# Expert layers in 32-token blocks on four column groups, blocks placed by expert rank in both layers, rows moved four blocks at a time

## The reference, cut to what matters

```python
grp = argmax(h @ w_coarse)                       # 1 of 4 groups
top_val, top_idx = top_k(fine logits of grp, 2)  # 2 of its 8 experts
gate = softmax(top_val) * w_grp
expert = grp * 8 + top_idx                       # 32 experts in all
def run_block(xe, e):                            # rows sent to expert e
    return (silu(xe @ w_gate[e]) * (xe @ w_up[e])) @ w_down[e]
y[token] += run_block(...) * gate                # each token gets 2 rows
```

## Time and profile before

| what | value |
| --- | --- |
| median of 3 timed runs | 1810.76 us (1804.28 to 1812.93) |
| the profiled execution | span 1805.0 us from first to last instruction; its time outside the span is not listed, and the three timed runs lie 0.7 us below to 7.9 us above this span |
| TensorE busy | 1687.1 us, 93% of the span |
| VectorE, ScalarE, GpSimd busy | 661.3, 448.8, 170.2 us |
| mean granted TensorE clock | 0.965 |
| moved by DMA | 519.45 MB, 288 GB/s over the span |
| layer 0, first turned block to last scatter | 353.4 to 875.8 us |
| layer 1, first turned block to last scatter | 1281.0 to 1776.1 us |

### The profile page before, as it was taken

How to read it: one execution, slowest core, us unless ns; L and a number is a source line. 1 busy time by engine, 2 the same in 40 slices (tenths; PEclk the granted TensorE clock), 3 DMA queues, 4 the chain that set the end, 5 groups by cost and what they waited for, 6 DMA issues and landing times.

```text
span 1805.0 us, 21821 instructions
## 1 busy us (share of the span) xinstructions
PE 1687.1 (93%) x8694; PEld 870.0 (48%) x8694; DVE 661.3 (37%) x1266; ACT 448.8 (25%) x807; POOL 170.2 (9%) x172
## 2 busy tenths in 40 slices
PE   7999999799999999999699998999699999999983
PEld 3455454445445555555345458965333333333331
DVE  3279341432222213122469846542522222221213
ACT  2233671133221112211448403332000000000001
POOL 0000000011111111110000113100111111111100
PEclk9999999799999999999899998999799999999996
DMA  9265531499999999999560181055899999999995
GB/s 366 98 238 183 195 133 47 141 401 408 394 408 408 403 411 403 403 413 394 191 239 1 25 124 48 1 211 219 317 397 403 398 409 406 406 416 413 420 421 197
DMA packets 95324, 519.45 MB, mean 288 GB/s; under 512 B 22509, under 2 KB 28237, under 8 KB 70648
## 3 DMA queue, kind: packets, MB, share of 16 engines
q1 hardware_dynamic: 84024, 500.66, 71.3%
q0 software_dynamic: 11200, 17.39, 2.9%
HBM read 508.19 MB, written 29.15 MB: 298 GB/s over the span
## 4 chain that ended last, share of the span: by engine, by line
PE 72%; DMA 12%; issue 8%; DVE 5%; ACT 2%; SPq 2%; DVEq 0%; POOLq 0%
PE bank L865 24%; PE bank L881 11%; PE bank L458 8%; PE bank L466 8%; DMA ring<-in_w_up 7%; PE bank L852 3%; PE bank L822 3%; PE bank L892 2%; PE bank L524 2%; PE bank L689 2%; PE bank L451 1%; DVE arena L2622 1%; PE bank L731 1%; DMA ring<-diag 1%; DMA arena<-xnd,smalli 1%
## 5 line engine op out<-in xcount | busy, mean ns | idle before, releaser
L867 PE MATMUL bank<-ring,arena 128*64 128x512 f32 x912 | 412.5, 606 | 0.0
L865 PE MATMUL bank<-ring,arena 128*64 128x512 f32 x896 | 402.5, 603 | 7.4 <-DMA ring<-in_w_up 4.9
L2521 DVE TENSOR_TENSOR arena<-arena,bank 64x512 f32<-64x512 f32 x70 | 48.3, 690 | 556.8 <-ACT arena L1815 556.8
L458 PE MATMUL bank<-arena,ring 128*128 128x512 f32 x560 | 244.6, 593 | 0.0
L865 PEld LDWEIGHTS bank<-ring,arena 128*64 128x64 f32 x896 | 119.6, 139 | 242.7 <-issue 236.0
L881 PE MATMUL bank<-ring,arena 128*64 128x512 f32 x424 | 195.0, 603 | 0.0
L883 PE MATMUL bank<-ring,arena 128*64 128x512 f32 x424 | 194.9, 603 | 0.0
L1815 ACT ACTIVATE arena<-bank 64x512 f32<-64x512 f32 x70 | 41.2, 588 | 509.6 <-PE bank L867 509.6
L1454 POOL DMA_INDIRECT arena<-xnd,smalli x70 | 67.6, 966 | 1052.6 <-PE bank L852 531.6
L458 PEld LDWEIGHTS bank<-arena,ring 128*128 128x128 f32 x560 | 105.4, 190 | 126.9 <-issue 126.9
L466 PE MATMUL bank<-arena 128*128 128x128 f32 x1008 | 126.8, 279 | 0.0
(11 more groups left out here) (441 smaller groups left out, 2110.0 us busy)
## 6 DMA issues: line engine op xcount, KB each, us to landing
ring<-in_w_up SPq DMA_DIRECT2D x53, 2048.0 KB, 19.1
ring<-in_w_gate SPq DMA_DIRECT2D x52, 2048.0 KB, 17.0
ring<-in_w_down SPq DMA_DIRECT2D x50, 2048.0 KB, 18.4
arena<-in_w_down SPq DMA_DIRECT2D x14, 2048.0 KB, 32.6
ring<-in_w_mod SPq DMA_DIRECT2D x12, 2048.0 KB, 15.3
arena<-in_w_gate SPq DMA_DIRECT2D x12, 2048.0 KB, 32.4
arena<-in_w_up SPq DMA_DIRECT2D x11, 2048.0 KB, 26.4
ring<-in_w_in SPq DMA_DIRECT2D x10, 2048.0 KB, 17.4
```

Source lines behind the costliest of these rows:

```text
L458: mm = pe.matmul(b[:, 0:n], w[:, k, col:col + P], ap[:, k, :], start=(k == 0), stop=(k == KD - 1))
L865: pe.matmul(GU[0:CAP, :], x, wg_[:, c, :], start=(c == 0), stop=(c == KD - 1), skip_group_check=True)
L867: mm = pe.matmul(GU[CAP:2 * CAP, :], x, wu_[:, c, :], start=(c == 0), stop=(c == KD - 1), skip_group_check=True)
```

## The change

- A block has 32 slots (`CAP = 32`). Four matmuls of a round write to PSUM partitions 0, 32, 64 and 96 on: gate and up with 256 columns each in two halves, down in four quarters. The stationary operand is 128 x 32.
- Both layers put experts into places by rank, with fixed sizes in blocks: layer 0 has 52 blocks, layer 1 has 56. `SIZES` gives the blocks of each place. Layer 0 now also does the ranking steps (`order`, `homes`) before its first gather, and loads experts 3 to 31 by a number read from the ranking.
- Gather and scatter work on four blocks (128 rows, a `QUAD`) at a time: 13 and 14 of each instead of 32 and 38. `xg` becomes one buffer. The transposes of a quad are done in two halves, one each after two of the blocks. Rows are scattered whole (4 KB). The routing weight moves from `take_y` of layer 1 to the final sum.
- `take_y` is four instructions of 32 x 256 instead of one of 128 x 512.
- `turn_h` is two transposes of 64 x 128 instead of four: the 64 partitions now hold the two 256-column halves of 32 rows.
- The context's 64 steps are spread over 98 slots.
- The down matrix is fetched in another row order: two runs of 8 KB per partition instead of one of 16 KB.
- The four small loads for layer 1's `m5`, `b5` become eight, moved ahead of the layer.

```diff
-CAP = 64
-NOV = 2 * T // CAP - 1
+CAP = 32
+QUAD = P // CAP
 FIXED = 3
-TWICE = 6
-BLOCKS = [[(p, 0) for p in range(NE)], []]
-TWICE_AT = {4 + 4 * i: FIXED + i for i in range(TWICE)}
-RANK = [TWICE_AT.get(p) for p in range(NE)]
-_rest = iter([*range(FIXED), *range(FIXED + TWICE, NE)])
-RANK = [next(_rest) if r is None else r for r in RANK]
-for _p in range(NE):
-    BLOCKS[1] += [(_p, h) for h in range(2 if _p in TWICE_AT else 1)]
+SIZES = [[2, 2, 2, 1, 1] + [2, 2, 1] * 8 + [2, 1, 1],
+         [2, 2, 2, 1, 1, 1] + [3, 1, 4, 1, 3, 1, 3, 1, 3, 1] + [2, 2, 1] * 4 + [2, 2, 1, 1]]
...
+BLOCKS = [[(p, h) for p in range(NE) for h in range(sizes[p])] for sizes in SIZES]
...
+CONTEXT_STEPS = 64
+CONTEXT_SLOTS = 2 * NB[0] - 6
...
+        def beside_now(k):
+            done, now = (min(i, CONTEXT_SLOTS) * CONTEXT_STEPS // CONTEXT_SLOTS for i in (k, k + 1))
+            return now > done
+
+        def turns_at(m, n):
+
+            b = n % QUAD
+            half = b - 2 if n < QUAD else b - 1
+            return half if half in (0, 1) and n // QUAD + 1 < NQ[m] else None
...
+                def turn_x(q, half):
+
+                    g = g0 + q
+                    bank = HT if q == 0 and half else XT
+                    if half == 0:
+                        pe.wait_ge(S("gathered"), 16 * (g + 1))
+                        positive(pe, S("xs_ready"), 2 * g)
+                    elif q:
+                        pe.wait_ge(S("xs_ready"), 2 * g + 1)
+                    for c in range(4):
+                        mm = pe.transpose(hd(bank, c), xg[:, 4 * half + c::KD], M["ident"])
                     mm.then_inc(S("xt_done"), 1)
...
-                    u, p = n % 2, BLOCKS[m][n][0]
+                    p, b, q = BLOCKS[m][n][0], n % QUAD, n // QUAD
                     wg_, wu_ = (home(m, j, p)[0] for j in range(2))
-                    pe.wait_ge(S("xs_ready"), n0 + n + 1)
+                    if b == 0:
+                        pe.wait_ge(S("xs_ready"), 2 * (g0 + q + 1))
                     if n == FIRSTB[m][p]:
                         for j in range(2):
                             pe.wait_ge(*home(m, j, p)[1])
                     for c in range(KD):
-                        x = xTs[u][:, CAP * c:CAP * c + CAP]
-                        pe.matmul(GU[0:CAP, :], x, wg_[:, c, :], start=(c == 0), stop=(c == KD - 1),
-                                  skip_group_check=True)
-                        mm = pe.matmul(GU[CAP:2 * CAP, :], x, wu_[:, c, :], start=(c == 0), stop=(c == KD - 1),
-                                       skip_group_check=True)
+                        x = xTs[q % 2][:, P * c + CAP * b:P * c + CAP * b + CAP]
+                        for i, (w, col) in enumerate(((wg_, 0), (wg_, 256), (wu_, 0), (wu_, 256))):
+                            mm = pe.matmul(GU[CAP * i:CAP * i + CAP, 0:256], x, w[:, c, col:col + 256],
+                                           start=(c == 0), stop=(c == KD - 1), skip_group_check=True)
                     mm.then_inc(S("gu_done"), 1)
...
-                    u, p = n % 2, BLOCKS[m][n][0]
+                    p = BLOCKS[m][n][0]
                     wd_, there = home(m, 2, p)
                     if n == FIRSTB[m][p]:
                         pe.wait_ge(*there)
                     pe.wait_ge(S("hts_ready"), n0 + n + 1)
                     positive(pe, S("y_taken"), n0 + n)
                     for c in range(4):
-                        x = hTs[u][:, CAP * c:CAP * c + CAP]
-                        pe.matmul(Y[0:CAP, :], x, wd_[:, c, 0:512], start=(c == 0), stop=(c == 3),
-                                  skip_group_check=True)
-                        mm = pe.matmul(Y[CAP:2 * CAP, :], x, wd_[:, c, 512:1024], start=(c == 0), stop=(c == 3),
-                                       skip_group_check=True)
+                        h, r = c // 2, c % 2
+                        x = hTs[:, 2 * CAP * r + CAP * h:2 * CAP * r + CAP * h + CAP]
+                        for i in range(4):
+                            mm = pe.matmul(Y[CAP * i:CAP * i + CAP, 0:256], x, wd_[:, c, 256 * i:256 * i + 256],
+                                           start=(c == 0), stop=(c == 3), skip_group_check=True)
                     mm.then_inc(S("y_done"), 1)
...
-                    u = n % 2
                     pe.wait_ge(S("h_done"), n0 + n + 1)
-                    for c in range(4):
-                        mm = pe.transpose(HT[:, CAP * c:CAP * c + CAP], hb[u][:, c::4], M["ident"][0:CAP, 0:CAP])
+                    for r in range(2):
+                        mm = pe.transpose(HT[:, 2 * CAP * r:2 * CAP * r + 2 * CAP], hb[:, r::2],
+                                          M["ident"][0:2 * CAP, 0:2 * CAP])
                     mm.then_inc(S("ht_done"), 1)
...
                 beside = iter(()) if m else context()
-                turn_x(0)
+                turn_x(0, 0)
+                turn_x(0, 1)
                 for n in range(last + 1):
                     gate_up(n)
                     if n == 0:
                         slots()
-                    if n >= ALONE:
+                    if beside_now(2 * n):
                         next(beside, None)
-                    if n < last:
-                        turn_x(n + 1)
+                    half = turns_at(m, n)
+                    if half is not None:
+                        turn_x(n // QUAD + 1, half)
                     if n == 0:
                         spots()
                     if n:
                         down(n - 1)
                     turn_h(n)
-                    if n >= ALONE:
+                    if beside_now(2 * n + 1):
                         next(beside, None)
                 down(last)
...
+            def split_down(w):
+                return w.rearrange("e (h p c) n -> e p h c n", h=2, c=2)
...
+                def gather(q):
+                    positive(pool, S("xt_done"), 2 * (g0 + q))
                     pool.indirect_dma_start(
-                        out=xg[u], out_offset=None, in_=xnd[m],
-                        in_offset=bass.IndirectOffsetOnAxis(ap=slots_any[:, n:n + 1], axis=0),
+                        out=xg, out_offset=None, in_=xnd[m],
+                        in_offset=bass.IndirectOffsetOnAxis(ap=slots_any[:, q:q + 1], axis=0),
                         bounds_check=T - 1, oob_is_err=False)\
-                        .then_inc(S(f"gathered{u}"), 16)
-
-                def scatter(n):
-                    u = n % 2
-                    pool.wait_ge(S("y_taken"), n0 + n + 1)
+                        .then_inc(S("gathered"), 16)
+
+                def scatter(q):
+                    u = q % 2
+                    pool.wait_ge(S("y_taken"), n0 + QUAD * q + QUAD)
                     pool.indirect_dma_start(
-                        out=halves, out_offset=bass.IndirectOffsetOnAxis(ap=homes_any[:, n:n + 1], axis=0),
-                        in_=ys[u], in_offset=None, bounds_check=4 * T - 1, oob_is_err=False)\
+                        out=yd[m], out_offset=bass.IndirectOffsetOnAxis(ap=homes_any[:, q:q + 1], axis=0),
+                        in_=ys[u], in_offset=None, bounds_check=2 * T - 1, oob_is_err=False)\
                         .then_inc(S(f"stored{u}"), 16)
 
-                for n in range(NB[m] + 2):
-                    if n == 2:
-                        pool.wait_ge(CV.free, CV.at(f"slots{m}"))
-                    if n < NB[m]:
-                        gather(n)
-                    if n == 4:
-                        pool.wait_ge(CV.free, CV.at(f"spots{m}"))
-                    if n >= 4:
-                        scatter(n - 4)
+                gather(0)
+                pool.wait_ge(CV.free, CV.at(f"slots{m}"))
+                gather(1)
+                gather(2)
+                pool.wait_ge(CV.free, CV.at(f"spots{m}"))
+                for q in range(3, NQ[m]):
+                    scatter(q - 3)
+                    gather(q)
+                scatter(NQ[m] - 3)
...
+                    b, q = n % QUAD, n // QUAD
                     act.wait_ge(S("y_done"), n0 + n + 1)
-                    positive(act, S(f"stored{q}"), 16 * ((n0 + n) // 2))
-                    A(ys[q], Y[:, :], ACT.Copy).then_inc(S("y_taken"), 1)
-
-                def step(n, beside):
-                    q = n % 2
+                    if b == 0:
+                        positive(act, S(f"stored{q % 2}"), 16 * stores(m, q))
+                    for i in range(4):
+                        ins = A(ys[q % 2][CAP * b:CAP * b + CAP, 256 * i:256 * i + 256], Y[CAP * i:CAP * i + CAP, 0:256],
+                                ACT.Copy)
+                    ins.then_inc(S("y_taken"), 1)
...
+                def affine_x(q, half):
+
+                    g = g0 + q
+                    bank, ks = HT if q == 0 and half else XT, slice(4 * half, 4 * half + 4)
+                    dve.wait_ge(S("xt_done"), 2 * g + half + 1)
+                    if q >= 2:
+                        dve.wait_ge(S("gu_done"), n0 + QUAD * (q - 1))
```

(34 more changed lines are left out.)

418 lines of the change are left out of this document (188 added, 230 removed).

## The result

The changed kernel takes 1839.78 us (median, 1834.45 to 1842.19) against 1810.76: ratio 1.0157, 95% interval 1.0131 to 1.0183. It is slower, by 29 us or 1.6%, and the profiled span grows by 33.6 us, from 1805.0 to 1838.6.

What follows compares the result with a forecast made beforehand. Layer 1 was taken as bound by DMA, layer 0 by DMA and TensorE at once; +17 us for layer 0 and -1 for layer 1 gave +16 on the median, 1827 us, own range 1815 to 1845, wider range 1798 to 1860.

Steps and rivals of the forecast that it cites:

- What bounds: Both layers: DMA bounds layer 1, DMA and TensorE together layer 0; TensorE's 85 and 135 us less work gain nothing.
- Start of layer 0: Ahead of layer 0's first gather: the layer now ranks experts first, +2.5 us.
- Down pieces in runs of 8 KB: Weight streams of both layers: shorter runs cost 0.1 us per down piece, +3 us a layer.
- The ring's loop: Layer 0's six weight buffers: refill loop of 17.95 us against 16.1 of cover, DMA idles 1.85, ten times: +18.5 us.
- The clock: Layer 0's loops: TensorE runs slower after idling for the down piece, 2.3 us lost in each of eight: +18 us.
- The rest of layer 0's stream: Layer 0's weights, rows and context's small packets: 493 of the stream's 506.6 us, which stay.
- Tail of layer 0: From layer 0's last landing to its last scatter: 5.2 us instead of 14.4.
- Layer 1: Layer 1 and the end: small loads -4, first buffers +3, down pieces +3, tail -3, final sums +0.5; together about -1 us.
- fewer us per MB of rows: Sign of being wrong, in the DMA queues: row price was taken to go with bytes, not packets, at 4.8 us per MB.
- Paying per indirect DMA: Rival, both layers: rows in fours are cheaper, saving 24 and 25 us of 40 a layer: 1778 us, chance 0.04.
- the ring never starves: Rival, layer 0: the loop fits its cover, so idle, clock and piece terms go: 1787 us, chance 0.10.
- No clock loss: Rival, layer 0: the 18 us for the slow clock drop out: 1809 us, no change, chance 0.20.

Runs made afterwards that it cites:

- e9: Kernel after, with 16 steps of small filling matmuls ahead of TensorE's wait for the down piece in each of layer 0's ten loops: 1837.6 us, ratio 1.0152.
- e2: Kernel after, with room for 15 overflow blocks instead of 31: 1826.65 us, ratio 1.0090.
- e8: e1 plus a branch around the five overflow loops, room for 31 kept: 1792.0 us, ratio 0.9909.
- e1: Kernel after, with each down piece of layer 0 queued right behind its own gate and up pieces: 1806.2 us, ratio 0.9983.
- e6: Kernel after, with each 4 KB result row scattered as two halves of 2 KB, by two indirect DMAs per quad: 1836.35 us, ratio 1.0139.
- e7: Kernel after, with two more indirect DMAs behind each scatter, all indices out of bounds: 1845.4 us, ratio 1.0186.
- e10: Kernel before, with a branch around its five overflow loops (room for 15): 1811.9 us, ratio 1.0019.

## Why the prediction was right, and where its sizes were off

The direction and the main mechanism hold. Slower was given 0.59, the time lies in the range of 1798 to 1860 and in the forecast's own range of 1815 to 1845. I added 16 us; 29 were measured, and 33.6 on the span that the terms were made for. Term by term, on the span:

- *What bounds.* Right. TensorE's busy time in the two streams fell by 40 us (504.0 to 463.9) and 98 (462.8 to 364.8), and none of it shows as a gain: layer 1's DMA share is 1.01, TensorE is idle 28% there (I said a quarter). The work fell by more, 85 and 135 predicted; the busy time also holds what the mean granted clock of 0.93 and 0.90 in the streams costs, 1.00 and 0.98 before. A gate_up takes 3.59 us to the start of what follows, 16 rounds of 0.224 where I took 0.217 from the earlier trace rows. Part of that is my rounding: 7.01 and 3.59 us for 24 rounds are 0.44 a round, not 0.43. The four column groups run side by side, and the 2.38x for three column groups of the Trainium skill (TensorE: Matmul & The Clock Gate, Measured speedup vs the span model) is not what this kernel shows: a block of 32 has the rounds of a block of 64 at half their length, 0.44 to 0.224, with twice the column groups.
- *Start of layer 0*: +2.5 predicted, +2.7 in the trace. Some of that comes from before the layer, since the same stretch starts between 351.3 and 357.5 in the kernels that differ only later.
- *Down pieces in runs of 8 KB*: +3 a layer. Measured too small to count: where nothing else moves, a gate piece lands 4.89 after the one ahead and a down piece 4.91 to 4.93 (4.88 before).
- *The ring's loop*: right in kind and place, the sum's mis-sized term. Predicted 1.85 + 2.3 us idle in each loop; measured 6.1 in the eight groups, and 4.5 in e9, where the slow product is nearly gone. So it is the 1.85, the loop by itself, that was too small. The loop from the down piece's landing to the next issue took 18.2 us, with 15.15 + 2.3 predicted: context 4.5 instead of 3.75 and a turn of 0.3, products of 1.86 and 3.59 instead of 1.73 and 3.47, the first of them 3.57 at the low clock, 0.3 to the issue. The lone piece landed 8.9 us after its issue, not 7.7. Small errors each, and together half again of the idle time, because the idle time is a difference: 27.1 us against 16.0 of cover and 4.9 of its own. The ten steps hold 57.5 us where I had 36.5.
- *The clock*: +18 predicted inside that. Right in kind, somewhat too large in size: the slow product is there in all eight groups (3.3 to 3.64 us for 1.93), and e9 gives a loop 1.6 us for it, 13 us in all.
- *The rest of layer 0's stream*: the other pieces take 5.25 us; 493 us and the down pieces over 92.5 would be 5.36. That gave some 9 us back. Last landing predicted 887.8, measured 902.8.
- *Tail of layer 0*: 14.5 to 5.9, predicted 5.2. Right.
- *Missed: the overflow loops.* The prediction has no term for them; it put them at nothing without a reason. I read the diff's 15 to 31 as room in tables, not as iterations that VectorE steps through between its last block and its next work. e2 gives them 12 us, and e8 beside e1 brings back 6.7 us between the layers and 6.3 at the end. This is the step that the prediction lacked.
- *Layer 1*: -1 predicted, of which +2 in the stream; measured -8.6 in the stream and -3.0 in the tail (as predicted). The DMA queues of two stretches of equal load, between 1295 and 1757 before, then between 1336 and 1790 after:

```profile
q1 hardware_dynamic: 12664, 179.57, 95.4%
q0 software_dynamic: 5680, 8.02, 5.2%
```

```profile
q1 hardware_dynamic: 16037, 179.61, 94.2%
q0 software_dynamic: 3744, 7.95, 4.6%
```

  The weights at 2.35 us per MB leave, of 462 and 454 us, 40.0 us for 8.02 MB of rows before and 31.9 us for 7.95 after, 5.0 and 4.0 us per MB. The difference is that of two large numbers (300 us of the kernel after gave 2.8 us per MB in e6's expectation), but fewer us per MB of rows was named as a sign of being wrong, and it showed. The argument that the row price goes with bytes and not with packets was circular: the row queue's share of the time, "a fifth", had been worked out from a price per MB. Paying per indirect DMA at 0.5 us is refuted by e7, and half rows as the cause by e6. At e7's 0.08 us, itself not shown, 48 fewer indirect DMAs would be 4 us of the 8, and the small loads that left the queue (predicted 4) would fit the rest; no run tests either by itself, so the cause of these 8 us stays open.

The sum of the measured terms: 2.7 + 38.7 - 8.6 + 8.3 - 8.6 - 3.0 + 4.2 = 33.7. I had 16. That the time still lies in the forecast's own range is in part luck: the missed 12 us of loops and the 15 us by which the stream of layer 0 was too short stand against 11 us that layer 1 gained beyond what I had; without that gain the time would have been some 1851, outside 1815 to 1845, though not outside 1798 to 1860.

The rival that the ring never starves (1787) is refuted by the steps; but e8, in which the loop is gone and the DMA share of layer 0 is 0.98, is near it at 1792. "No clock loss" would have been 1809, and e9 shows why it can't be: with the slow product nearly gone the loop is still 4.5 us too long. Of the other signs, the DMA share of layer 0 fell to 0.91 (0.93 to 0.95 predicted) and its last scatter moved to 908.7 (893).

## What to carry to other kernels

Halving a block's time does not only free the fast engine: it moves the point at which buffers come free against the order in which their refills are queued. Walk each loop of the kind "this piece lands, these products follow, that buffer is refilled" and set it beside the transfers that are queued meanwhile; if it is longer, the difference is lost once a turn, and the cure may be an order (one rule of the queue, 31 us here) and no speed at all. And look in a diff for trip counts that follow from a block size: iterations that do nothing are paid where that engine ends last (e2, e8), and cost nothing where another wait ends later (e10).

## What was not expected of the hardware

- An empty iteration of a loop with a branch costs VectorE 0.5 us (15.46 us for 31; 8.5 us less with 16 fewer), and none of it appears as busy time.
- An indirect DMA whose 128 indices are all out of bounds costs GpSimd 0.98 us to issue, like a full one, but the stream of weights 0.08 us at most as far as one trace shows (e7).
- Rows of 4 KB written as two halves of 2 KB cost the stream nothing that the trace shows (482.4 us for layer 1's stream in e6, 482.0 in the kernel after).
